# Light experts as one item with whole rows, and the order of items within a pair

## The reference, cut to what matters

```python
def swiglu(h, w_gate, w_up, w_down):
    return (jax.nn.silu(h @ w_gate) * (h @ w_up)) @ w_down

def moe_swiglu(h, w_router, b_router, w_gate, w_up, w_down):
    logits = h @ w_router + b_router
    top_v, top_i = lax.top_k(logits, 2)
    top_w = softmax(top_v)
    gates = sum(one_hot(top_i, 8) * top_w[..., None], axis=-2)
    out = 0
    for e in range(8):
        out = out + gates[..., e:e + 1] * swiglu(h, w_gate[e], w_up[e], w_down[e])
    return out
```

## Time and profile before

| | us |
|---|---|
| median of 3 runs | 1721.28 |
| lowest and highest | 1719.71, 1722.2 |
| the profiled execution | 1721.49 |
| its span, first to last instruction | 1719.8 |

### The profile page before, as it was taken

How to read it: one execution, slowest core, us unless ns; L and a number is a source line. 1 busy time by engine, 2 the same in 40 slices (tenths; PEclk the granted TensorE clock), 3 DMA queues, 4 the chain that set the end, 5 groups by cost and what they waited for, 6 DMA issues and landing times.

```text
span 1719.8 us, 25435 instructions
## 1 busy us (share of the span) xinstructions
PE 1625.6 (95%) x10722; PEld 903.4 (53%) x10722; DVE 647.6 (38%) x1501; ACT 354.6 (21%) x766; POOL 73.3 (4%) x147
## 2 busy tenths in 40 slices
PE   6999999989999999998997979999999999999985
PEld 3665544368888864443785764334434433343432
DVE  4987972474545521507589362000100010001001
ACT  4334452221101100003546342000100000000001
POOL 2210100000000030000011000000000000000000
PEclk9999999989999999998999979999999999999998
DMA  8503633443333153226143319999999999999997
GB/s 314 159 14 111 242 109 125 162 119 77 98 99 89 47 89 96 73 98 245 50 124 100 98 50 412 411 412 405 412 413 411 400 412 413 409 406 410 410 411 285
DMA packets 186064, 396.31 MB, mean 230 GB/s; under 512 B 34371, under 2 KB 104619, under 8 KB 170842
## 3 DMA queue, kind: packets, MB, share of 16 engines
q1 hardware_dynamic: 180576, 391.23, 61.8%
q0 software_dynamic: 4112, 3.34, 1.3%
q10 hardware_dynamic: 1258, 0.07, 0.0%
HBM read 389.36 MB, written 1.05 MB: 227 GB/s over the span
## 4 chain that ended last, share of the span: by engine, by line
PE 88%; DVE 4%; DMA 3%; ACT 2%; SPq 1%; issue 1%; ACTq 0%; DVEq 0%
PE ps L1073 85%; PE ps L1076 3%; DMA ring<-in_w_in_dram 1%; DVE norms L1987 1%; DMA ring<-in_moe_w_down_dram 1%; SPq L579 1%; DMA ring<-in_moe_w_gate_dram 1%; DVE aT L1995 0%; DVE work L2004 0%; ACT dg L741 0%; ACT work L732 0%; ACT work L733 0%; DVE hT L2009 0%; ACT work L848 0%; DVE aT L2221 0%
## 5 line engine op out<-in xcount | busy, mean ns | idle before, releaser
L1073 PE MATMUL ps<-ring,work 128*32 128x256 f32 (+5 forms) x3368 | 404.2, 488 | 11.3 <-DMA ring<-in_moe_w_down_dram 7.0
L1073 PEld LDWEIGHTS ps<-ring,work 128*32 128x32 f32 (+2 forms) x3368 | 155.4, 118 | 250.8 <-issue 209.0
L1073 PE MATMUL ps<-work 128*64 128x64 f32 (+11 forms) x2348 | 232.5, 326 | 9.1 <-DVE work L2271 5.1
L1073 PE MATMUL ps<-work,ring 128*128 128x512 f32 (+1 forms) x656 | 237.0, 514 | 1.3 <-DVE work L2303 1.3
L1073 PE MATMUL ps<-aT,ring 128*128 128x256 f32 (+1 forms) x800 | 235.3, 443 | 2.9 <-ACT aT L805 2.2
L2458 DVE TENSOR_TENSOR work<-work,ps 128x768 f32<-128x768 f32 (+5 forms) x27 | 18.8, 706 | 525.3 <-PE ps L1073 525.3
L1073 PEld LDWEIGHTS ps<-work 128*64 128x64 f32 (+5 forms) x2348 | 157.7, 150 | 74.5 <-issue 58.8
L1073 PEld LDWEIGHTS ps<-aT,ring 128*128 128x128 f32 x800 | 152.3, 192 | 72.6 <-issue 54.4
L1073 PE MATMUL ps<-aT,work 128*128 128x256 f32 (+6 forms) x1148 | 185.4, 466 | 4.5 <-DMA aT<-in_moe_w_down_dram 4.5
L1073 PEld LDWEIGHTS ps<-work,ring 128*128 128x128 f32 x656 | 124.5, 190 | 106.4 <-issue 98.5
L1073 PEld LDWEIGHTS ps<-aT,work 128*32 128x32 f32 (+2 forms) x1148 | 105.3, 143 | 70.7 <-issue 48.4
(11 more groups left out here) (360 smaller groups left out, 1291.2 us busy)
## 6 DMA issues: line engine op xcount, KB each, us to landing
ring<-in_moe_w_up_dram SPq DMA_DIRECT2D x55, 1024.0 KB, 16.3
ring<-in_moe_w_down_dram SPq DMA_DIRECT2D x51, 1024.0 KB, 15.6
ring<-in_w_ada_dram SPq DMA_DIRECT2D x23, 2048.0 KB
ring<-in_moe_w_gate_dram SPq DMA_DIRECT2D x37, 1024.0 KB, 15.2
ring<-in_moe_w_up_dram SPq DMA_DIRECT2D x28, 768.0 KB, 16.7
aT<-in_moe_w_gate_dram SPq DMA_DIRECT2D x17, 1024.0 KB, 15.6
aT<-in_moe_w_down_dram SPq DMA_DIRECT2D x17, 1024.0 KB, 17.3
ring<-in_moe_w_gate_dram SPq DMA_DIRECT2D x18, 768.0 KB, 16.3
```

The costliest lines, as they stand in the source:

```text
L1073: return pe.matmul(o, lhs, rhs, start=start, stop=stop)
```

## The change

1. **Items.** A light or tiny expert is one item with all 2816 columns. In each of the first three pairs the order is chunks 0, 1, 2 of the large expert and then the light one; the last pair is rank 3's three chunks, then tiny. There are 16 items for 24 (`PER = 4`).
2. **Blocks of a light or tiny expert.** Gate and up come as eight blocks each, 128 whole rows in a block: one piece of 11264 bytes for each partition, 1.44 MB in all. Its down matrix comes as 11 blocks; for a light expert ten are of row pairs (8192 bytes) within the halves of the 2816 rows, and the last takes the 128 left-over rows of each half, as two pieces of 4096 bytes.
3. **Places.** `aT` and `ring` are one stretch, `arena`, of 20480 words. An allocator, run when the program is built, goes round in it with a head; a block of 2048 words may take `norms` or `Sg` instead when these were used longest ago. Each block waits for the last block whose words it takes, and for block n-16 (16 semaphores).
4. **Matmuls.** A light gate block is one k with 1408 columns for each half: 512, 512 and 384, in PSUM banks 0, 1, 7 for gate and 2, 3, 4 for up. A tiny one is 11 matmuls of 256 columns in groups of 32.
5. **hs and hTs** have one buffer each. Transposes of a light item come in three parts, those of tiny in two. The carries of the last sums into PSUM stand between the last up's blocks 4 to 7.

The diff, cut to its core:

```diff
-        items = [(r, c) for pair in PAIRS[:-1] for c in range(NC) for r in pair]
-        items += [(r, c) for r in PAIRS[-1] for c in range(NC)]
+        items = []
+        for a, b in PAIRS[:-1]:
+            items += [(a, 0), (a, 1), (a, 2), (b, 0)]
+        items += [(LAST, c) for c in range(NC)] + [(TINY, 0)]
         NI = len(items)
-        ALONE = NI - NC
+        PER = NI // len(PAIRS)
+        ALONE = NI - 1
...
+        def chunk(i):
+            return CHUNK[items[i][1]] if big(i) else (0, FE)
...
+        def rows_per_block(i):
+            return 2 if big(i) else 1
...
         def parts(i):
-            return 2 if big(i) else 1
+            return 2 if big(i) or tiny(i) else 3
...
-        NBUF = 12
...
+            sizes += [rows_per_block(i) * (1024 if big(i) else FE)] * blocks_in(i)
+            gate_end.append(len(sizes))
             if i:
+                sizes += [2 * D] * (width(i - 1) // 256)
+                down_end.append(len(sizes))
...
+        NSEM = 16
+        LATE_FROM = 20
+        ARENA = KC * T + 4 * SLOT
+        cell = 256
+        places, after = [], []
+        taken = {"arena": [-1] * (ARENA // cell), "norms": [-1], "Sg": [-1]}
+        head = KC * T // cell
+        for n, size in enumerate(sizes):
+            need_cells = size // cell
+            if head + need_cells > ARENA // cell:
+                head = 0
+            options = [(max(taken["arena"][head:head + need_cells]), 0, "arena")]
+            if size == 2 * D:
+                options.append((taken["norms"][0], 1, "norms"))
+                if n >= LATE_FROM:
+                    options.append((taken["Sg"][0], 2, "Sg"))
+            prev, _, where = min(options)
+            if where == "arena":
+                places.append((where, head * cell))
+                taken[where][head:head + need_cells] = [n] * need_cells
+                head += need_cells
+            else:
+                places.append((where, 0))
+                taken[where][0] = n
+            after.append(max(prev, n - NSEM))
...
-                    elif m >= EARLY:
-                        sp.wait_ge(sem("block_used"), n + 1 - (EARLY if m < LATE_FROM else NBUF))
+                    if after[m] >= 0:
+                        sp.wait_ge(sem("block_used"), ph * n_blocks + after[m] + 1)
...
+                    rows = P * rows_per_block(i)
+                    for d in range(blocks_in(i)):
+                        load(n, w[0, bass.ds(expert[items[i][0]], 1), rows * d:rows * d + rows, f0:f0 + width_], "e (k p) n -> p (e k) n")
...
-                        act.activation(hTs[:, i % 2, t:t + nt, 0:rows],
+                        act.activation(hTs[:, t:t + nt, 0:rows],
...
+                    if not big(i):
+                        if bank == 0 and not tiny(i) and p0 + i // PER:
+                            for g in range(2):
+                                pe.wait_ge(sem(f"y_ready{g}"), 2 * (p0 + i // PER))
+                        for k in range(KC):
+                            pe.wait_ge(block_in(n), landed_at(n))
+                            b = wblock(n)
...
+                                lhs = xg[:, k, SLOT0[r]:SLOT0[r] + HP]
+                                for part, o in enumerate((0, 1, 7) if bank == 0 else (2, 3, 4)):
+                                    lo, hi = 512 * part, min(512 * part + 512, FE // 2)
+                                    for g in range(2):
+                                        last = mm(ps[HP * g:HP * g + HP, o, 0:hi - lo], lhs,
+                                                  b[:, 0, FE // 2 * g + lo:FE // 2 * g + hi], k == 0, k == KC - 1)
+                            last.then_inc(sem("block_used"), 1)
+                            n += 1
+                            between(k)
...
                     def turn_last(d):
-                        if i and (d == 0 if big(i - 1) else d == 1):
-                            turn_h(i - 1, 0)
-                        if i and big(i - 1) and d == 1:
-                            turn_h(i - 1, 1)
+                        if i and d < parts(i - 1):
+                            turn_h(i - 1, d)
```

More of the change, by code:

```diff
@@ new lines, in block_in, with landed_at @@
+        def block_in(n):
+            return sem(f"block_in{n % NSEM}")
+        def landed_at(n):
+            return 16 * (n // NSEM + 1)
+        def wblock(n):
+            where, at_ = places[n % n_blocks]
+            size = sizes[n % n_blocks]
+            if where == "arena":
+                b = arena[:, at_:at_ + size]
+            else:
+                b = norms[:] if where == "norms" else Sg.rearrange("p i r s -> p (i r s)")
+            return b.rearrange("p (k n) -> p k n", k=1 if size == FE else 2)
@@ new lines, in load_down @@
+                def load_down(n, i):
+                    f0, w = chunk(i)
+                    one = moe_down[0, bass.ds(expert[items[i][0]], 1), f0:f0 + w, :]
+                    split = not big(i) and not tiny(i)
+                    for d in range(w // 256):
+                        if not split:
+                            src = one[:, 256 * d:256 * d + 256, :]
+                        elif d < FN // 2 - 1:
+                            at_ = FE // 2 * (d // 5) + 256 * (d % 5)
+                            src = one[:, at_:at_ + 256, :]
+                        if split and d == FN // 2 - 1:
+                            load(n, one.rearrange("e (h r) n -> r (e h) n", h=2)[FE // 2 - P:FE // 2], "p k n -> p k n")
+                        else:
+                            load(n, src, "e (p k) n -> p (e k) n" if row_pairs(i, d) else "e (k p) n -> p (e k) n")
+                        n += 1
+                    return n
@@ L582, in experts @@
                 for i in range(NI):
-                    r, c = items[i]
-                    f0, w = CHUNK[c]
+                    r = items[i][0]
                     if r not in expert:
                         expert[r] = sp.value_load(by_rank[0:1, r:r + 1], min_val=0, max_val=NE - 1)
[L587 to L590, removed]
+                    n = load_in(n, i, moe_gate)
@@ L591, in experts @@
                     if i:
[L592 to L604, removed]
+                        n = load_down(n, i - 1)
@@ L1571, in project_in @@
                                            b[:, j, w // 2 * g:w // 2 * g + w // 2], k == 0, k == KC - 1)
[L1572 to L1582, removed]
+                        if heavy(i):
                             last.then_inc(sem("block_used"), 1)
@@ L1610, in project_out @@
                             t = 2 * d + j
-                            first, end = c == 0 and t == 0, c == NC - 1 and t == tiles - 1
+                            first, end = c == 0 and t == 0, final and t == tiles - 1
                             h, u = divmod(t, blocks)
@@ L1708, in experts @@
                     n = project_in(n, i, 2, spread_last)
-                turn_h(NI - 1, 0)
+                for j in range(parts(NI - 1)):
+                    turn_h(NI - 1, j)
                 project_out(n, NI - 1)
@@ L2451, in experts @@
                             copy_y(ended)
-                        for q in range(3):
+                        for q in range(3 if i < ALONE else 4):
                             add(ended, q)
```

188 lines of the change are left out of this document (102 added, 86 removed).

## The result

| | median us | runs |
|---|---|---|
| before, on the same chip | 1720.49 | 1719.54 to 1722.2 |
| changed | 1742.35 | 1740.45 to 1744.57 |

The changed kernel takes 1.0124 times as long, 95% interval 1.0109 to 1.0139: 21.3 us more (18.8 to 23.9). The forecast was 1738, range 1729 to 1748. Its profiled execution took 1741.21 us with a span of 1739.5.

The account below looks back on a forecast made before the run. The prediction took DMA and PE, joined by a buffer, to bound the expert stage. From 1719.8, adding 27.4 us of DMA idling and subtracting 10.6 for whole rows gave span 1736.6 (other way 1736.2); mean plus 1.5: 1738 us, range 1729 to 1748.

Parts of the forecast that it names:

- Two machines joined by a buffer: Expert stage: DMA delivers at 410 GB/s, PE works without idle until 1656.6, and only buffer depth keeps either from stopping.
- A: PE from 1046.35 through the first light block at 1132.8; block 38 issued at 1132.9, DMA idle 10.6 us.
- B: Blocks 38 to 66: 82.1 us of transfer, over at 1216.8; PE waits for block 66 until 1217.3, lag zero.
- The restart: After an empty stream, a load's bytes start 1.8 us after issue; possibly 4.3 each, 5 us more for two.
- C: PE from block 66 through light block 95: 102.2 us, to 1319.5; block 101 then issued, DMA idle 16.8 us.
- D: Blocks 101 to 247: 398.7 us, to 1720.1, no stop in pairs three and four; last block late, 1723.5.
- Part 1, whole rows: Light gate and up blocks take 3.38 us each at 426 GB/s; gain 10.6 us if nothing else moved.
- Parts 2 and 3: Order: PE falls back through three whole chunks before a light expert repays; allocator: seven light places, 20 us cover, not 30.7.
- The buffers did not hide the order: Faster rival: buffers hide the order, PE's lag in the heavy expert staying under about 24 us; 1710.8 us, chance 0.09.
- the packets did speed up: Rival judged here: 11264-byte rows are cut back as 4096-byte ones were, so packets do not speed up; 1745 us, chance 0.13.
- the third: Rival: PE's clock falls in the light experts while it waits for DMA; 1743 us, chance 0.12.

Follow-up runs that it names:

- e4_less_pe: Changed kernel with half of the columns left out of the large experts' main matmuls, so part of the computation is missing; loads, order and places as changed: 1710.32 us.
- e1_order_only: Kernel before with one line changed: the large expert's three chunks stand ahead of the light one's three; blocks and twelve places as before: 1736.82 us.
- e2_split_rows: Changed kernel with each whole row of a light or tiny expert's gate and up loaded by three DMAs of 4096, 4096 and 3072 bytes: 1747.0 us.
- e6_less_pe_split: e4_less_pe with whole rows loaded by three DMAs as in e2_split_rows; part of the computation is left out: 1722.14 us.
- e8_order_nine: e1_order_only with light or tiny gate and up loads waiting for the block nine before them instead of twelve: 1746.92 us.
- e5_wide_chunks: Kernel before, twelve places and interleaving kept, but light or tiny experts in chunks of 2048 and 768 columns, the first in 8192-byte packets: 1715.89 us.

## Why the prediction was right, step by step

**What bounds the kernel.** Two machines joined by a buffer: right. With PE's work cut (e4_less_pe) the order and the places cost nothing; with the order alone (e1_order_only) 15 us of transfer are already lost.

**A**, right to 0.1 us: block 38's load was issued at 1132.99, forecast 1132.9. The stop before it is 10.4 for 10.6. The 0.1 is in part luck: PE began 0.2 us earlier than taken (1046.16), and the item's transposes were some 0.6 us shorter than summed, against blocks that were a little longer.

**Where the stops lie** was wrong. The forecast let the loads of blocks 0 to 37, and later 67 to 100, run at full rate to their end and put one idle piece behind them, 1124 to 1135 and 1305 to 1321. The trace has 412 GB/s in the first of these. The missing step is that the light blocks before 38 and 101 wait for PE as well: the first light gate's load is issued at 1111.56, in the rows above, after 27 GB/s in 1105 to 1110, and its last at 1135.98; in the second stop the rate is 0 in 1295 to 1300, and 353 in 1305 to 1321, where the forecast had nothing moving. So the engines run dry earlier and in several pieces. The sum did not suffer, since it hangs on the last of these waits, the one for the use of block 32 or 95, and on PE's work up to there.

**B**, the term that was mis-sized: PE met block 66 at 1219.6, forecast 1217.3. The stretch has 415 GB/s from 1135 to 1275; 1120 to 1140, at its start, is at 393, with a queue of a few light blocks. The restart was taken as one pause of 1.8 us; as the loads wait for PE one by one, there are several small ones. In B e2_split_rows is no later than the changed kernel (block 66 at 1219.63 and 1219.56), so the whole rows' gain there, some 1.6 us, did not arrive. e2_split_rows moves 404 GB/s in 1120 to 1140 where the changed kernel moves 393; that the gain went into these pauses is likely and was not tried by itself.

**C**, 100.7 us from there to the issue of block 101 at 1320.29, forecast 102.3. The heavy blocks took what was summed; the transposes did not: a group of four of the heavy expert's takes 0.46 us (1240.24 to 1240.70; 0.47 in the trace of before, 1268.12 to 1268.59), and the five groups of C are 2.5 us for the 4.7 summed. The price of 1.4 to 1.6 us an item was read from a medium expert's rows, with drain added. The second stop is 16.3 for 16.8. The early and the late error cancel to 0.7 us.

**D**, PE met the last block at 1726.0, forecast 1723.5; 0.7 of this is C's, 1.8 are D's own in 400, and the runs don't say where. The end took 13.5 us for 12.7, since the last matmuls ran at the lower clock (1.93 for 1.07 us). Span 1739.5 for 1736.4, and the median stands 2.9 us above it, where before's 1.5 was taken: 4.3 us in all over the forecast. So the change cost 21.3 us where the sum had 16.7.

**Part 1, whole rows.** 3.38 us a block was right: 426 GB/s in a stretch with light up blocks alone, and 10.3 us between e4_less_pe and e6_less_pe_split for 10 by the fit. The highest rate of any 10 us is 429.
The Trainium skill (DMA: Bandwidth & Descriptors, Bandwidth) has 435 GB/s as the fabric's ceiling; the trace agrees so far as nothing in it is above.

**Parts 2 and 3.** By the runs the loss splits in 15 us for the order (e1_order_only), 10 for the shorter cover (e8_order_nine, e2_split_rows), and about 5, give or take 4, that the whole rows give back, where 8 were expected for the blocks behind the first stop.

**The rivals.** The buffers did not hide the order; the packets did speed up; PE's clock read 1.00 in every 10 us between 1030 and 1700, the light experts' short waits included, so the third had no part. Pairs three and four never stopped the DMA engines, as D has it: no ten us between 1320 and 1720 are under 403 GB/s.

## What to carry to other kernels

In a stage where the DMA rate is the bound and the compute engine is nearly as busy, the order of heavy and light work decides how far the engine falls behind, and the cover is bytes of buffer ahead of it; sum the engine's work minus the transfer's over the longest run of heavy items and compare it with the buffer before making the transfers faster. The last wait that holds back a load gives the sum; where the engines stand needs the wait of every load ahead of it too. Larger packets gave 3 to 4% of the rate here; take them in a form that keeps the places and the interleaving (e5_wide_chunks). Read a nearly empty queue in the issue-to-landing time and in GB/s.

## What was not expected of the hardware

A DMA queue that is almost empty need not look idle. In e1_order_only this stretch has a share of 1.01 and moves 359 GB/s:

```profile
1282.00:1290.00 8.00, 8.00 (x25) 4.39 (x24) 0.00 (x0) 1.41 (x2) 0.00 (x0) 1.00 1.01 359
```

Its loads issued in 1262 to 1300 landed soon after issue, by the same kernel's DMA line:

```profile
DMA to landing us min/median/max: 4.2/4.9/8.1
```

And PE's short waits for light blocks in the changed kernel (0.71 and 0.81 us in the rows above) stand in stretches with a granted clock of 1.00, the 2.4 GHz level throughout, while behind the longer waits at the very end, 1.3 to 1.5 us each, it read 0.66 in 1720 to 1730, a mix with the 1.2 GHz level:

```profile
1720.00:1730.00 10.00, 6.95 (x64) 2.56 (x64) 0.59 (x2) 0.54 (x2) 0.00 (x0) 0.66 0.25 105
```
